# A hybrid decoder on 8 cores: decay logits packed into parts of the array, wider pooling bands, sample states in pairs, and another order of the first loads

## The reference, cut to what matters

```python
proj = xn @ w_in
q, k, v, gz, og, u, ga, gb = split(proj)        # gz has 16 columns, q and k 512, the others 1024
log_a = log_sigmoid(gz @ w_gk_up + b_gk) / 16   # (B, T, 4 heads, 128)
o, s_new = gla_chunked(q, k, v, log_a, s0)      # in it, per chunk and head:
    o = attn @ v + (q * exp(b)) @ S
    S = exp(b_end) * S + k_dec.T @ v            # S is 128 x 256 per head
...
# pooling: channel groups 0 to 3 take the mean of the last 2, 4, 8, 16 tokens
d = win / cnt - u
y = (d @ w_mix) * scale
merged = sig(ga) * (o @ w_branch_a) + sig(gb) * (y @ w_branch_b)
h = x + merged @ w_out                          # then cross attention over 256 memory tokens, then an MLP
```

## Time and profile before

| what | value |
|---|---|
| three timed runs | 1295.19, 1295.45, 1297.27 us; median 1295.45 |
| the profiled execution | 1297.27 us, span 1295.4 us (core 1) |
| spans of the cores | 1287.2 to 1295.4 us |
| mean granted TensorE clock of the cores | 0.993 to 0.995 |
| busy share of the span: PE, DVE, ACT, POOL | 97%, 51%, 50%, 5% |

### The profile page before, as it was taken

How to read it: one execution, slowest core, us unless ns; L and a number is a source line. 1 busy time by engine, 2 the same in 40 slices (tenths; PEclk the granted TensorE clock), 3 DMA queues, 4 the chain that set the end, 5 groups by cost and what they waited for, 6 DMA issues and landing times.

```text
span 1295.4 us, 23430 instructions; the slowest of 8 cores (1287.2 to 1295.4 us)
## 1 busy us (share of the span) xinstructions
PE 1261.3 (97%) x8602; PEld 647.8 (50%) x8602; DVE 655.3 (51%) x1088; ACT 650.8 (50%) x1333; POOL 69.1 (5%) x131
## 2 busy tenths in 40 slices
PE   8999899999999999999999999899999999999997
PEld 6445555444455544444544455544455544454453
DVE  5644764232467754444675356523244754444346
ACT  4556866555687741123245288655558753120304
POOL 2100000000000000000000010000100000000000
PEclk9999999999999999999999999899999999999999
DMA  9999478363658668697779694838862333342403
GB/s 194 185 183 167 70 132 172 47 117 91 170 135 218 130 169 146 109 160 152 153 172 169 109 152 99 159 71 144 138 191 41 60 63 66 65 83 52 95 1 138
DMA packets 33675, 160.93 MB, mean 124 GB/s; under 512 B 4598, under 2 KB 5246, under 8 KB 22156
## 3 DMA queue, kind: packets, MB, share of 16 engines
q0 software_dynamic: 18112, 104.29, 49.7%
q1 hardware_dynamic: 15452, 55.15, 12.6%
HBM read 241.63 MB, written 22.80 MB: 204 GB/s over the span
## 4 chain that ended last, share of the span: by engine, by line
PE 86%; DMA 9%; issue 2%; DVE 1%; ACT 1%; DVEq 0%; SPq 0%; POOL 0%; ACTq 0%; POOLq 0%
PE pb L818 78%; PE pb L829 5%; PE pb L849 3%; DMA wt_46<-wscratch 2%; DMA wt_45<-wu 1%; DMA wscratch<-bpt_54 1%; DMA land_113<-xp 1%; DMA s0f_121<-sgla 1%; DMA xsF<-xs 1%; DMA xst_91<-xp 1%; PE pb L839 1%; DMA sgs<-s0f_121 1%; DMA xst_94<-xp 0%; ACT xn_102 L868 0%; DVE S L889 0%
## 5 line engine op out<-in xcount | busy, mean ns | idle before, releaser
L889 DVE SCALAR_TENSOR_TENSOR xh<-pb,r_178,xh 128x512 f32<-128x512 f32 x128 | 95.6, 750 | 91.0 <-PE pb L818 90.6
L818 PE MATMUL pb<-actT,wt_45 128*128 128x512 bf16 x448 | 101.4, 379 | 0.0
L818 PE MATMUL pb<-actT,wt_44 128*128 128x512 bf16 x448 | 100.4, 379 | 0.0
L868 ACT ACTIVATE tmp_98<-pb 128x512 f32<-128x512 f32 (+1 forms) x48 | 28.3, 590 | 111.2 <-PE pb L818 108.7
L818 PE MATMUL pb<-actT,wtG 128*128 128x512 bf16 x320 | 72.8, 379 | 0.0
L818 PE MATMUL pb<-actT,wt_43 128*128 128x512 bf16 x320 | 72.5, 379 | 0.0
L818 PEld LDWEIGHTS pb<-actT,wt_45 128*128 128x128 bf16 x448 | 43.0, 98 | 50.6 <-issue 0.4
L818 PEld LDWEIGHTS pb<-actT,wt_44 128*128 128x128 bf16 x448 | 43.2, 98 | 49.6
L878 DVE TENSOR_TENSOR xh<-pb,xh 128x512 f32<-128x512 f32 x64 | 44.1, 689 | 46.6 <-PE pb L818 46.2
L868 ACT ACTIVATE tmp_95<-pb 128x512 f32<-128x512 f32 (+1 forms) x49 | 28.5, 582 | 74.9 <-PE pb L818 59.8
L818 PE MATMUL pb<-wt_45,actT 128*128 128x512 bf16 x256 | 59.3, 379 | 0.6 <-DVE xn_101 L889 0.4
(11 more groups left out here) (559 smaller groups left out, 2376.1 us busy)
## 6 DMA issues: line engine op xcount, KB each, us to landing
wt_44<-wu POOLq DMA_DIRECT2D x19, 1024.0 KB, 10.9
wt_43<-wu POOLq DMA_DIRECT2D x17, 1024.0 KB, 11.8
wt_45<-wu POOLq DMA_DIRECT2D x17, 1024.0 KB, 12.6
wt_46<-wu POOLq DMA_DIRECT2D x16, 1024.0 KB, 11.2
wtG<-wu POOLq DMA_DIRECT2D x13, 1024.0 KB, 10.9
xh<-xp SPq DMA_DIRECT2D x16, 512.0 KB
yp<-xh SPq DMA_DIRECT2D x15, 512.0 KB, 5.6
wt_46<-wscratch SPq DMA_DIRECT2D x2, 1024.0 KB, 26.2
```

The source lines that it names most:

```text
L818: ins = e.matmul(out, l, r, start=(start and i == 0), stop=(stop and i == m - 1))
L868: return self.g.op("act", lambda e: e.activation(out=out, in_=in_, func=func, scale=scale, **kw), reads=rd, writes=wr, cost=c)
L889: return self.g.op(eng, lambda e: e.scalar_tensor_tensor(out=out, in0=in0, scalar=scalar, in1=in1, op0=op0, op1=op1), reads=rd, writes=[ou ...
```

## The change

1. **Forget gate.** `wgz` is padded to 32 columns. `gzp` now makes 32 matmuls per tile instead of 16: four column groups of 32 columns each take one quarter of the tokens (256), so that the four quarters of `gzT` lie in four groups of 32 partitions. `decay` makes 16 matmuls of 32 rows and 256 columns, in four row groups and four banks at a time, instead of 8 of 16 rows and 512 columns; ACT's first exponential is 16 operations of 256 columns instead of 8 of 512.
2. **Pooling.** A block's band now reaches 16 columns into the next block (144 columns): 5 matmuls per bank instead of 8.
3. **Sample states in pairs.** Sequences i and i+8 go together. One mask serves both; their outer products take 32 rows each, in two row groups, into two banks. The mask is computed ahead of the loads into the pair's buffers, and loads wait for it. There are still four buffers, which are now two pairs.
4. **Start.** The warm-up is 28 groups, all at the front. x1 and x2 each wait for a warm-up group, later blocks x_s for x_(s-2). v1's weight waits for x4 instead of x5. `wgk` and two small constants wait for nothing, the samples wait for x6 instead of x7. `pmf` may be loaded 30 instead of 18 us ahead.

The argument `par` of `mms` and `mmx` divides the planner's cost only.

```diff
+    c["pmx"] = np.ascontiguousarray(np.concatenate([pm[:, 0], pm[:, 1, :, :16]], axis=2))
...
-        bk[b * ST:(b + 1) * ST, b] = 1.0
+        bk[b * ST:(b + 1) * ST, b % 8] = 1.0
...
-            self.dma("pool", flat, self.I["wu"][UNITS[name][0]], nb=5.0, ahead=ahead, after=self.xld[5:6] if k == 1 else self.xld[7:] if 1 < k < 5 else ())
+            self.dma("pool", flat, self.I["wu"][UNITS[name][0]], nb=5.0, ahead=ahead, after=self.xld[4:5] if k == 1 else self.xld[7:] if 1 < k < 5 else ())
...
-        warm = []
-        for i in range(42):
-            self.g.pri_off = 0 if i < 24 else 40
-            warm.append(self.mm(self.pb[b][:64, :64], [(self.zero[:, :], self.zero[:, :])] * 8))
-        self.g.pri_off = 0
+        warm = [self.mm(self.pb[b][:64, :64], [(self.zero[:, :], self.zero[:, :])] * 8) for i in range(28)]
         d("sp", self.cols[:], I["cols"][:, :])
         d("pool", self.ident[:], I["c_ident"][:, :])
         xl = []
         for s in range(8):
-            xl.append(d("sp", self.xst[s][:, :], I["xp"][s * 128:(s + 1) * 128, :], after=() if s < 2 else warm[23:24] if s < 5 else xl[s - 3:s - 2]))
+            xl.append(d("sp", self.xst[s][:, :], I["xp"][s * 128:(s + 1) * 128, :], after=() if s == 0 else warm[14:15] if s == 1 else warm[20:21] if s == 2 else xl[s - 2:s - 1]))
         self.xld = xl
...
-        x = self.xld[6:7]
+        x = self.xld[5:6]
         d("pool", self.wgz[:].rearrange("p k n -> p (k n)"), I["wgz"][:, :], after=x)
-        d("pool", self.wgk[:], I["wgk"][:, :], after=x)
-        d("pool", self.rst512[:], I["c_rst512"][:, :], after=x)
-        d("pool", self.rst64[:], I["c_rst64"][:, :], after=x)
+        d("pool", self.wgk[:], I["wgk"][:, :])
+        d("pool", self.rst512[:], I["c_rst512"][:, :])
+        d("pool", self.rst64[:], I["c_rst64"][:, :])
...
         def gzp():
-            for hf in range(2):
-                b = self.bank()
-                self.mm(self.pb[b][:16, :], [(self.wgz[:, kc, :], A[:, kc, hf * 512:(hf + 1) * 512]) for kc in range(8)])
-                self.cp("act", self.gzT[:, hf * 512:(hf + 1) * 512], self.pb[b][:16, :])
+            b = self.bank()
+            self.mmx([(self.pb[b][32 * j:32 * j + 32, :256], self.wgz[:, kc, :], A[:, kc, j * 256:(j + 1) * 256], kc == 0, kc == 7)
+                      for kc in range(8) for j in range(4)], par=3.0)
+            self.cp("act", self.gzT[:, :], self.pb[b][:, :256])
...
         def decay():
             for h in range(4):
-                for hf in range(2):
-                    b = self.bank()
-                    self.mm(self.pb[b][:, :], [(self.wgk[:, h * 128:(h + 1) * 128], self.gzT[:, hf * 512:(hf + 1) * 512])])
-                    self.act(T1[:, h, hf * 512:(hf + 1) * 512], self.pb[b][:, :], AF.Exp, scale=-1.0, bias=self.ncols[:, h:h + 1])
+                if h % 2 == 0:
+                    bs = [self.bank() for _ in range(4)]
+                    self.mms([(self.pb[bs[j]][:, x * 256:(x + 1) * 256],
+                               [(self.wgk[32 * j:32 * j + 32, (h + x) * 128:(h + x + 1) * 128], self.gzT[32 * j:32 * j + 32, :])])
+                              for x in range(2) for j in range(4)], par=2.5)
+                for j, b in enumerate(bs):
+                    self.act(T1[:, h, j * 256:(j + 1) * 256], self.pb[b][:, (h % 2) * 256:(h % 2 + 1) * 256], AF.Exp, scale=-1.0,
+                             bias=self.ncols[:, h:h + 1])
                 self.act(T1[:, h, :], T1[:, h, :], AF.Ln, bias=self.ncols[:, 5:6])
...
+                pr = (self.ublk(ti, hf * 4) + 8) % 9
                 items = []
+                if not (first and hf == 0):
+                    items.append((self.pb[b][:, :16], self.ur[:, pr, csl], self.pmx[:, g, 128:]))
                 for s4 in range(4):
-                    s = hf * 4 + s4
-                    cu = self.ublk(ti, s)
-                    pr = (cu + 8) % 9
-                    o = self.pb[b][:, s4 * 128:(s4 + 1) * 128]
-                    l = self.ur[:, cu, csl]
-                    if first and s == 0:
-                        items += [(o, l, self.pm23[:, 0, g, :], True, False), (o, l, self.pm23[:, 1, g, :], False, True)]
+                    o = s4 * 128
+                    l = self.ur[:, self.ublk(ti, hf * 4 + s4), csl]
+                    if first and hf == 0 and s4 == 0:
+                        items += [(self.pb[b][:, :128], l, self.pm23[:, 0, g, :]), (self.pb[b][:, :128], l, self.pm23[:, 1, g, :]),
+                                  (self.pb[b][:, 128:144], l, self.pmx[:, g, 128:])]
                     else:
-                        items += [(o, l, self.pm01[:, 0, g, :], True, False),
-                                  (self.pb[b][:, s4 * 128:s4 * 128 + 16], self.ur[:, pr, csl], self.pm01[:, 1, g, :16], False, True)]
+                        n = 144 if s4 < 3 else 128
+                        items.append((self.pb[b][:, o:o + n], l, self.pmx[:, g, :n]))
+                items = [x + (i == 0, i == len(items) - 1) for i, x in enumerate(items)]
                 self.mmx(items)
                 self.cp("act" if (cc + hf) % 2 else "dve", self.dT[:, cc, hf * 512:(hf + 1) * 512], self.pb[b][:, :])
...
-        self.dma("sp", self.pmf[:, :], I["wpmT"][:, :], ahead=18.0)
+        self.dma("sp", self.pmf[:, :], I["wpmT"][:, :])
...
-        self.dma("sp", self.xsF[:, :, :].rearrange("p k t -> p (k t)"), self.I["xs"][:, :], after=self.xld[7:8])
+        self.dma("sp", self.xsF[:, :, :].rearrange("p k t -> p (k t)"), self.I["xs"][:, :], after=self.xld[6:7])
...
-        for i in range(SB):
-            sf = self.ring("s0f", self.s0f)
-            sb_ = self.ring("s0b", self.s0b)
+        for i in range(SB // 2):
+            pair = (i, i + 8)
+            sf = [self.ring("s0f", self.s0f) for _ in pair]
             kb = self.ring("kblk", self.kblk)
-            self.dma("sp", sf[:, :, :].rearrange("p h v -> p (h v)"), I["sgla"][i], nb=1.4)
-            self.cp("act", sb_[:, :, :], sf[:, :, :])
-            self.ts("dve", kb[:, :], self.kdts[:, :], self.bmk[:, i:i + 1], ALU.mult, also=[sf[:, :, :]])
-            self.mmx([(self.pb[ob][:, j * 64 + i * ST:j * 64 + (i + 1) * ST], sb_[:, j // 2, (j % 2) * 128:(j % 2 + 1) * 128],
-                       self.qs[:, j // 2, i * ST:(i + 1) * ST], False, i == SB - 1 and j == 7) for j in range(8)])
+            self.ts("dve", kb[:, :], self.kdts[:, :], self.bmk[:, i:i + 1], ALU.mult, also=[f[:, :, :] for f in sf])
+            for k, n in enumerate(pair):
+                self.dma("sp", sf[k][:, :, :].rearrange("p h v -> p (h v)"), I["sgla"][n], nb=1.4)
+            for k, n in enumerate(pair):
+                sb_ = self.ring("s0b", self.s0b)
+                self.cp("act", sb_[:, :, :], sf[k][:, :, :])
+                self.mmx([(self.pb[ob][:, j * 64 + n * ST:j * 64 + (n + 1) * ST], sb_[:, j // 2, (j % 2) * 128:(j % 2 + 1) * 128],
+                           self.qs[:, j // 2, n * ST:(n + 1) * ST], False, n == SB - 1 and j == 7) for j in range(8)])
+            yield
             for hp in range(2):
-                b = self.bank()
-                self.mms([(self.pb[b][:, (h % 2) * 256:(h % 2 + 1) * 256],
-                           [(kb[:, h * 128:(h + 1) * 128], self.vts[:, h * 256:(h + 1) * 256])]) for h in (2 * hp, 2 * hp + 1)])
-                for h in (2 * hp, 2 * hp + 1):
-                    self.stt("dve", sf[:, h, :], sf[:, h, :], self.eBs[:, h, i:i + 1], self.pb[b][:, (h % 2) * 256:(h % 2 + 1) * 256],
-                             ALU.mult, ALU.add)
-                if hp == 0:
-                    yield
-            self.dma("sp", O["sgs"][i], sf[:, :, :].rearrange("p h v -> p (h v)"), nb=1.4)
+                bs = [self.bank() for _ in pair]
+                hs = (2 * hp, 2 * hp + 1)
+                self.mms([(self.pb[bs[k]][:, (h % 2) * 256:(h % 2 + 1) * 256],
+                           [(kb[32 * k:32 * k + 32, h * 128:(h + 1) * 128], self.vts[32 * k:32 * k + 32, h * 256:(h + 1) * 256])])
+                          for h in hs for k in range(2)], par=1.8)
+                for h in hs:
+                    for k, n in enumerate(pair):
+                        self.stt("dve", sf[k][:, h, :], sf[k][:, h, :], self.eBs[:, h, n:n + 1],
+                                 self.pb[bs[k]][:, (h % 2) * 256:(h % 2 + 1) * 256], ALU.mult, ALU.add)
+                    if hp == 0:
+                        yield
+            for k, n in enumerate(pair):
+                self.dma("sp", O["sgs"][n], sf[k][:, :, :].rearrange("p h v -> p (h v)"), nb=1.4)
```

More of the change, by code:

```diff
@@ L568, in __init__ @@
         inp("ckT", [SB, 128, 2048]); inp("cv", [SB, 128, 2048])
-        inp("wu", [NU, 128, 4096]); inp("wgz", [128, 128]); inp("wgk", [16, 512]); inp("wpmT", [128, 2048])
+        inp("wu", [NU, 128, 4096]); inp("wgz", [128, 256]); inp("wgk", [128, 512]); inp("wpmT", [128, 2048])
         inp("cols", [128, NCOL]); inp("g_fin", [D])
@@ L820, in mm, with mms @@
```

(12 more changed lines are left out.)

19 lines of the change are left out of this document (9 added, 10 removed).

## The result

The changed kernel takes 1302.3 us (median of four runs, 1300.4 to 1306.1) against 1295.7 for the kernel before on the same chip: a ratio of 1.0052, with a 95% interval of 1.0028 to 1.0076. It is slower by about 6.6 us. The profiled execution took 1300.4 us; its slowest core is core 3, with a span of 1298.6 us.

The account below looks back on a forecast made before the run. PE was taken as the bound (86% of the chain, busy 97% of the span). Terms 3.3 - 3.6 - 2.8 + 3.7 + 2.5 = +3.1 on the profiled 1297.3 gave 1300.4, less 1.8 for the median: 1298.6 us, range 1290 to 1307.

Parts of the forecast that it names:

- A, the start: Start up to k: v1's weight `wt_44` lands late behind pmf, PE waits, clock drops; +3.3 us, ends -1.5 and +7.5.
- B, the gate: Second tile's forget gate and decay: four strips run at once, 1.9 us instead of 5.5; -3.6 us, ends -4.2 and 0.
- my price for a narrow group: PE's cost of entering and leaving a narrow matmul group: 0.10 us at each side, 0.20 for entry and exit.
- rival 1: Gate, decay and states: strips run one after the other, so the packing gains are lost; 1309.3 us, slower, chance 0.10.
- C, the bands: Pooling with wide bands: fewer matmuls -1.8 us, and -1 from the pauses; -2.8 us in all.
- the limit: Second tile's pooling: evictions alternating on DVE and ACT empty a bank every 0.32 us at best.
- the pauses: Pooling: pauses of 5.2 and 1.9 us without releaser, 9.1 with the clock's 2.0; -1 counted, ends 0 and -9.
- The old price: Pooling before the change: six banks (48 matmuls) take 2.09 us, 0.35 each.
- rival 4: Pooling: the pauses, from PE's own instruction supply, vanish; 9.1 us, of which 1 counted; 1290.5 us, faster, chance 0.10.
- D: Sample states: outer products in pairs -0.25 us, waits for loads as two buffers turn together +3.9; +3.7, ends -0.3 and +11.
- E: Weights behind the states: PE waits 1.5 us for `wt_43` before the MLP, 1.0 for `wtG`; +2.5, ends 0 and +5.

Follow-up runs that it names:

- old_start: The changed kernel with the whole start of the kernel before (warm-up, block waits, v1's weight, constants, pmf): 0.9991, 1294.5 us.
- warmup_only: The changed kernel with old block waits, v1's weight after x5 and pmf 18 us ahead; short warm-up and early constants stay: 0.9995, 1295.1 us.
- gate_pool: The kernel before with the packed gate and decay and the wide pooling bands alone: 0.9906, 1283.5 us.
- buffers: `old_start` with the four state buffers dealt so that one pair takes both halves of the room wtG needs: 0.9937, 1287.5 us.
- early: `old_start` with the state loads allowed 60 instead of 30 us ahead: 0.9975, 1292.5 us.
- pairs_only: The kernel before with the sample states in pairs alone: 1.0085, 1306.7 us.

## Why the prediction was right, and where it was wrong

The forecast was slower, 1298.6 us in a range of 1290 to 1307; measured is 1302.3. The side and the largest risk, the start, were right; the amount was half, and the terms were off in both directions.

**A, the start: the size met partly by luck, the mechanism only in part.** Without the gate's own 3.6 us the term meant a loss of 6.9 us; measured are 7.9, give or take 3.6. At k the new start is 10.7 us behind `old_start` as a mean (67.3 and 56.6) and 9.8 at the first band matmul of the second tile; it is 6.3 at the end, as in that pooling only two cores of the changed kernel pause, and all eight of `old_start`. `pmf` did stand where the order says, `wt_44` was issued at 30.34 us on the slowest core (27.8 predicted; 27.9 on core 0) and landed 13.3 us later, at 43.7 (40.8 predicted). But the step "`wt_44` lands late, and PE waits for it" holds on two cores only, which wait 2.8 and 3.7 us for it. On two others, the slowest among them, PE waits longer for x6. I had the blocks behind `pmf` but took them as moving on at 1.8 us each; x6 ran beside the weight and took 13.7 us on core 3, under 6.2 on core 0. And a wait that is the same on all eight cores, 4.25 us for x1, I did not see at all: it comes from ACT's queue, in which x1's norm stands behind the eviction of a group that waits for the weight. The orders that I read were those of PE and SP. The clock was a cost, as said, but not behind a hole at the weight: it is low from 13 us on (0.66 over 13 to 33 us) in every kernel with the short warm-up, `warmup_only` included, and I had given the warm-up no term.

**B, the gate: right, a little small.** 1.65 us were measured where 1.9 were predicted. The difference is in my price for a narrow group: the rows give 0.10 us for going in and out together (1.62 against 1.51), and I charged 0.20. With 0.10 three times it is 1.6. The strips do run at once, and rival 1 falls. The 32 matmuls of the gate run 3.5 times as fast as 16 x 0.216 us, the way in and out contained. The eight decay matmuls take 0.33 us where 8 x 0.108 = 0.86 would be one after the other, 2.6 times as fast. The Trainium skill, "TensorE: Matmul & The Clock Gate", part 3 ("Measured speedup vs the span model"), has 3.07 for four row strips of 512 columns: the trace gives less for 256 columns with the entry counted, and more than its 2.38 for three column strips, as there are four here.

**C, the bands: the gain about right, the limit wrong, the pauses underrated.** Banks follow each other at 0.27 us in the second tile, the price of their columns; over these six the evictions did not hold PE at 0.32. The old price was too high by the run-out of the last matmul (0.35, by starts 0.32), so the gain is 0.05 a bank, 1.7 us over 32 banks where 1.8 were counted: two errors that met. The bands alone gave 7.6 us, and the gate alone 17.0 where 7.2 were predicted for both tiles. The larger part of the difference is the pause, of which I counted 1 of 9.1 us. What rival 4 describes happened with either part alone, and on six of eight cores of the changed kernel. I had held against it that nothing in the change touches the place of the pause; the runs show that the place moves with what stands ahead of it.

**D and E, the pairs: the sign right, the size at half.** Predicted were +6.2, measured +11.0. PE's work was not the cost: four outer products took 0.32 us instead of 0.43, so 16 groups save 1.8 us where I had 0.25, again for the doubled price (3.45 with 16 x 0.10 is 1.85 less than 6.9), and rival 1 has no ground here either. The Trainium skill, "TensorEngine Tiling (Array Packing)", "Key Properties", says that a change of mode drains the engine; the 0.10 us beyond 2 x 0.108 = 0.22 agrees with a price of that size, but for a whole group, not at each side of it. The step that fell short is E. Its two waits came as worked out on the slowest core (1.51 for 1.5, 1.03 for 1.0), and a third, for `mTs`, with them. They are the visible end of an order of weights that the planner chose with a buffer in `wtG`'s room stored last. Dealing the buffers otherwise gave back 7.0 us, give or take 2.7. D was predicted as late loads at every turn of a pair; what the traces show is one place, the casts of the first pair in ACT's queue, with 1.3 to 3.1 us for `mT` on the eight cores of the changed kernel (2.9 on the slowest), and small waits of 0.3 to 0.8 us behind it. At the later turns no cast of the slowest core waits for its load, which was a sign of being wrong. The traces part the rest by place. Against `gate_pool`, `old_start` is level up to the end of the first tile's pooling, 5.1 us later at the first outer product (352.3 and 357.4 as means) and 8.8 at the MLP's first matmul (494.7 and 503.5). `buffers` has the same 5.0 at the first place and 3.9 at the second: what it mends lies behind the first outer product, and what is left was lost before it. So D's 3.7 was met in size by another cause, and E's 2.5 was half of the 4.9 that `buffers` gives back at the MLP. `early` is 3.5 ahead of `old_start` at the first outer product, and 2.5 at the end.

**The sum.** It was 3.1 and measured 6.7, as the gains were 12.2 where 10.0 had been predicted, the pairs cost 4.8 more and the start 1.0 more. Two errors on one side met one on the other. Each of these steps holds a share of the pause in the second tile's pooling, which no term of the sum could place.

## What to carry to other kernels

An order of instructions is read on every engine that stands between a load and the matrix engine: a norm that queues behind an eviction waits for that eviction's weight, and no list of loads shows it. Work that only fills PE's waits is not always idle work: in the kernels without the 14 zero groups between the blocks PE had 0.57 to 0.74 of its clock from 13 to 33 us, where it had 0.83 to 1.00 with them. When buffers are taken in pairs, look at which of them shares its room with the next stage, and let that one be stored first; here one tuple was worth 7 us. Where a change holds parts that gain and parts that lose, build each alone: the packed gate by itself ran at 1278.7 us, 17 us better than the kernel before, and was the best kernel of this study.

## What the runs showed of the hardware that I had not expected

In the kernel before all eight cores pause at the same instruction of the second tile's pooling, 2.8 to 5.2 us, with nothing that they wait for. The kernel with the packed gate alone, whose work at that place is the same, loses it on all eight cores, and so does the one with the wide bands alone; with both parts seven cores have a pause of 1.6 to 4.1 us among the bands, and in the changed kernel two cores one of 3.6.

What stands beside every pause is a packet of the instruction queue. Of the list of DMA queues for the pause of the earlier trace rows, 829 to 835 us on core 1 (packets, MB, share of 16 engines):

```profile
q8 instruction: 1, 0.02, 1.0%
```

That packet (16 KB) runs from 832.5 to 833.4 us, and PE goes on at 834.9. In all 14 kernels together the second tile's pooling has 63 pauses of more than 1 us without a releaser, and each of them ends 1.1 to 1.7 us after such a packet has ended. Between two packets PE starts some 250 matmuls and weight loads (the median of every kernel). So PE most likely waits for its own code there, as rival 4 supposed; and a place counted in instructions would move with any change ahead of it, as it did: in `pairs_only`, with the same code at the place, the pause lies four matmuls later on all seven cores that have one. That is an argument from the traces: no run changed the number of instructions alone, and why some kernels have their code in time (none of the 16 cores of the two with one part pauses) stays open. The stretch has a DMA share of 0.94.
